# A routed two-layer block on one core: the router reads raw sums, token remainders move to TensorE and ScalarE

## The reference

```
x = layernorm(ALPHA * x + attention(x), ln_g[layer, 0], ln_b[layer, 0])
f = grouped_moe(x, router_w, router_b, w_gate, w_up, w_down)
x = layernorm(ALPHA * x + f, ln_g[layer, 1], ln_b[layer, 1])

def grouped_moe(x, ...):
    scores = sigmoid(x @ router_w)                 # 256 x 32
    sel = scores + router_b                        # choose by these
    # the group of 4 experts whose two best sum highest, then its two best experts
    gate = scores of the two, divided by their sum
    y += gate_e * ((silu(x @ w_gate[e]) * (x @ w_up[e])) @ w_down[e])   # e chosen for the token
```

## Time and profile before

| | us |
|---|---|
| three runs | 733.11, 728.86, 729.58 |
| median | 729.58 |
| the profiled execution | 729.95 |
| its span, first to last instruction | 728.1 |
| mean granted clock of TensorE | 0.984 |
| busy in the span: TensorE, VectorE, ScalarE, GpSimd | 686.7, 335.1, 211.2, 129.5 |

### The profile page before, as it was taken

The page is one execution under the profiler, slowest core; times in us unless marked ns, Lnnn a source line. Parts: engine busy times, 40 slices in busy tenths (PEclk is TensorE's granted clock), DMA queues, the critical chain, the costliest instruction groups (busy, mean ns, idle before and its releaser), DMA issues. The chain is left out here.

```text
span 728.1 us, 10053 instructions
## 1 busy us (share of the span) xinstructions
PE 686.7 (94%) x3657; PEld 382.6 (53%) x3657; DVE 335.1 (46%) x672; ACT 211.2 (29%) x416; POOL 129.5 (18%) x141
## 2 busy tenths in 40 slices
PE   7999999879999999999989898988999999999993
PEld 5979778453334343345546776845433434334551
DVE  4758654753433324233264755585343432323226
ACT  4568661312111111111155135341211111111111
POOL 4004010140201010010019560015120101001000
PEclk9999999999999999999999999999999999999998
DMA  8980058929999999999995019393999999999991
GB/s 310 385 338 2 1 216 368 406 85 361 420 421 422 421 421 421 421 424 420 423 417 232 1 33 421 131 387 111 367 421 421 420 422 421 423 420 423 420 413 66
DMA packets 40360, 237.65 MB, mean 326 GB/s; under 512 B 3825, under 2 KB 4257, under 8 KB 15233
## 3 DMA queue, kind: packets, MB, share of 16 engines
q1 hardware_dynamic: 39408, 235.64, 79.5%
q10 hardware_dynamic: 576, 1.05, 0.5%
q0 software_dynamic: 336, 0.44, 0.2%
HBM read 236.06 MB, written 1.05 MB: 326 GB/s over the span
## 5 line engine op out<-in xcount | busy, mean ns | idle before, releaser
L572 PE MATMUL psum<-ring,work 128*64 128x512 f32 (+2 forms) x1296 | 234.0, 512 | 7.2 <-DVE work L1981 7.2
L572 PEld LDWEIGHTS psum<-ring,work 128*64 128x64 f32 (+1 forms) x1296 | 95.5, 140 | 143.0 <-issue 119.7
L572 PE MATMUL psum<-ring,scratch 128*64 128x512 f32 x512 | 116.9, 598 | 3.7 <-ACT scratch L1440 3.7
L2023 DVE TENSOR_TENSOR scratch<-psum,scratch 128x256 f32<-128x256 f32 x32 | 13.6, 425 | 183.2 <-ACT scratch L1436 183.2
L2099 POOL COPY work<-work 128x512 f32 x60 | 39.0, 651 | 316.5 <-PE psum L572 307.6
L1429 ACT ACTIVATE x_T_rounded<-psum,small 128x512 fp32r<-128x512 f32 x64 | 43.8, 687 | 110.2 <-DVE scratch_rounded L2004 75.8
L572 PEld LDWEIGHTS psum<-ring,scratch 128*64 128x64 f32 x512 | 33.9, 136 | 68.8 <-issue 63.6
L1436 ACT ACTIVATE scratch<-psum 128x256 f32<-128x256 f32 x32 | 12.3, 384 | 195.1 <-PE psum L572 195.1
L572 PE MATMUL psum<-ring_rounded 128*128 128x256 f32 (+1 forms) x214 | 66.5, 311 | 0.0
L572 PE MATMUL psum<-ring_rounded,x_T_rounded 128*128 128x512 f32 x192 | 60.6, 396 | 0.0
L572 PE MATMUL psum<-x_T_rounded,scratch_rounded 128*128 128x512 f32 x128 | 56.7, 443 | 0.9 <-issue 0.7
(11 more groups left out here) (247 smaller groups left out, 845.9 us busy)
## 6 DMA issues: line engine op xcount, KB each, us to landing
ring<-in_moe_w_gate SPq DMA_DIRECT2D x64, 1024.0 KB, 15.4
ring<-in_moe_w_up SPq DMA_DIRECT2D x64, 1024.0 KB, 19.6
ring<-in_moe_w_down SPq DMA_DIRECT2D x64, 1024.0 KB, 20.2
ring<-in_diff_w_qkv SPq DMA_DIRECT2D x5, 2048.0 KB, 19.9
ring<-in_diff_w_o SPq DMA_DIRECT2D x1, 4096.0 KB, 14.5
ring<-in_mla_w_o SPq DMA_DIRECT2D x1, 4096.0 KB, 35.9
ring<-in_mla_w_q_b SPq DMA_DIRECT2D x1, 2304.0 KB, 29.5
ring<-in_mla_w_kv_b SPq DMA_DIRECT2D x1, 2048.0 KB, 28.0
```

Source lines behind the costliest of these rows:

```text
L572: return pe.matmul(dst, lhsT, rhs, start=start, stop=stop, skip_group_check=True)
L2023: dve.tensor_tensor(h_sb, psum[:, 6, FF:2 * FF], act_s, ALU.mult).then_inc(m["h_ready"], 1)
```

## The change

- **Raw sums to the router.** TensorE transposes `xs` before it is normalised, as soon as the addition of a tile is done (`z_ready`), each tile into two banks of its own. ScalarE and VectorE copy one bank each of a tile (`raw_copy`) without scale and shift. No zero matmuls stand ahead of the transposes.
- **The norm on the logits.** The router's weights are multiplied by the norm's scale (`rw_scaled`) and by its shift, and both are summed by column (`router_rows`); a product with ones spreads the sums to all tokens. A logit becomes `rstd` times the raw one, plus the shift's sum, minus mean times `rstd` times the scale's sum: two VectorE instructions a tile, the second ahead of the sigmoid.
- **Normalisation later.** ScalarE normalises tile 0 after the logit copy and tile 1 after the sigmoid, each whole; VectorE's half is gone.
- **Remainders.** `tok_hi` and `tok_lo` keep the tokens' own order of columns; the casts read without a step, and the sort takes every eighth column as its stationary operand. TensorE forms `xs` times the identity (fp32) plus `hi` times the negative identity in two banks, and ScalarE copies that to `tok_lo`. VectorE's three subtractions are gone. `TOP_WAIT` is 6 instead of 28.
- **Diagonals.** `tok_lo[1]` lies where `diag` lies, so GpSimd now waits for the whole sort (`sort_ps`) before it writes `diag`.
- **Queues.** The router's weights are issued by GpSimd behind the squares (layer 0) and behind the split weights (layer 1). SyncE reads the overflow count of layer 0 into a register ahead of the attention's loads instead of behind them.

```diff
-START_WAIT, FIRST_WAIT, TOP_WAIT, SORT_WAIT = 14, 8, 28, 8
-NORM_WAIT = {1: (8, 4), 2: (11, 0), 3: (8, 4)}
+RAW_BANKS = ((4, 5, 2, 3), (4, 5, 6, 7))
+ROW_BANK = (6, 3)
+REST_BANK = (4, 6)
+START_WAIT, FIRST_WAIT, NORM_WAIT, TOP_WAIT, SORT_WAIT = 14, 8, (11, 0), 6, 8
...
-            load_router(0)
+            sp.wait_ge(*at[0]("o_ps", HEADS))
             load_down(0, 0, 0)
...
+            more = overflows(sp, 0)
             sp.wait_ge(*mo[0]("gu_ps", 14))
...
# TensorE, moe(l)
-                transpose_x(2 * l + 1)
-                pe.wait_ge(ld_rw, 16 * (l + 1))
+                for t in range(TT):
+                    pe.wait_ge(z_ready, TT * l + t + 1)
+                    for half in range(2):
+                        for k in range(4):
+                            last = pe.transpose(psum[:, RAW_BANKS[l][2 * t + half], k * P:(k + 1) * P],
+                                                xs[:, t, 4 * half + k::KD], ident)
+                        last.then_inc(xt[2 * l + 1]["ps"], 1)
+                mm(psum[:, ROW_BANK[l], 0:2 * EXPERTS], ones, routing()["rows"], True, True).then_inc(m["lg_ps"], 1)
+                pe.wait_ge(*x_copied(2 * l + 1))
...
-                    last = mm(psum[rows, 0, 0:SEQ], rw[:, k, :], xT[:, k, :], k < 4, k >= 4)
+                    last = mm(psum[rows, 0, 0:SEQ], rw_scaled[:, k, :], xT[:, k, :], k < 4, k >= 4)
...
-                keep_clock(TOP_WAIT)
+                for t in range(TT):
+                    banks = [psum[:, REST_BANK[t] + c, :] for c in range(2)]
+                    cols = [slice(c * 512, (c + 1) * 512) for c in range(2)]
+                    pe.wait_ge(*ln[2 * l]("norm", (1, 3)[t]))
+                    for c in range(2):
+                        mm(banks[c], ident, xs[:, t, cols[c]], True, False)
+                    pe.wait_ge(*m("hi_ready", t + 1))
+                    for c in range(2):
+                        last = mm(banks[c], minus_ident[:, :], tok_hi[t][:, cols[c]], False, True)
+                    last.then_inc(m["lo_ps"], 1)
+                keep_clock(TOP_WAIT, 0)
...
-                    for half, part in enumerate(xs_parts(t, k)):
-                        last = mm(psum[:, SORT_BANKS[k], :], part, onehot_r[:, t, :],
+                    for half, part in enumerate((tok_hi[t], tok_lo[t])):
+                        last = mm(psum[:, SORT_BANKS[k], :], part[:, k::KD], onehot_r[:, t, :],
...
+                pe.wait_ge(*m("lo_ready", TT))
                 for t in range(TT):
-                    pe.wait_ge(*m("hi_ready", t + 1))
                     pe.wait_ge(*m("hot_ready", t + 1))
-                    pe.wait_ge(*m("lo_ready", t + 1))
...
# ScalarE, moe(l)
-                act_xt(2 * l + 1)
+                root(n, 0)
+                raw_copy(0)
+                root(n, 1)
+                raw_copy(1)
                 act.activation(small[:, 60:61], eps[:, :], ACT.Sigmoid)
-                act.wait_ge(*m("lgt_ps", 1))
-                act.copy(logit_T, psum[:, 0, 0:SEQ]).then_inc(m["lgt_sb"], 1)
-                act.wait_ge(*m("lg_ps", 1))
-                act.activation(routing()["score"], psum[:, 1, 0:64], ACT.Sigmoid).then_inc(m["score"], 1)
-                act.wait_ge(*ln[2 * l]("norm", 3))
+                act.wait_ge(*m("lg_ps", 2))
+                act.copy(logit_T, psum[:, 0, 0:SEQ]).then_inc(m["router_act"], 1)
+                normalise(0)
+                act.wait_ge(*m("logit", TT))
+                act.activation(routing()["score"], routing()["sel"], ACT.Sigmoid).then_inc(m["router_act"], 1)
+                normalise(1)
+                act.wait_ge(*ln[n]("norm", 3))
                 act.wait_ge(*m("hi_ready", 1))
-                act.copy(hi_1, xs_tiles(1, 0, KD)).then_inc(m["hi_ready"], 1)
+                act.copy(tok_hi[1], xs[:, 1, :]).then_inc(m["hi_ready"], 1)
+                for t in range(TT):
+                    act.wait_ge(*m("lo_ps", t + 1))
+                    act.copy(tok_lo[t], psum[:, REST_BANK[t]:REST_BANK[t] + 2, :].rearrange("p c n -> p (c n)"))\
+                       .then_inc(m["lo_ready"], 1)
...
# VectorE, raw_layer_norm (new; router_rows(l) is called just before it)
+                statistics(n, 1)
+                raw_copy(0)
+                raw_copy(1)
+                scales(n, 1)
+                dve.wait_ge(*ln[n]("rstd", TT))
+                dve.wait_ge(*m("lg_ps", 1))
+                row = c["rows"]
+                chain(dve.tensor_copy(row, psum[:, ROW_BANK[l], 0:2 * EXPERTS]))
+                for t in range(TT):
+                    part = slice(t * EXPERTS, (t + 1) * EXPERTS)
+                    last = dve.scalar_tensor_tensor(out=c["masked"][:, part], in0=row[:, 0:EXPERTS],
+                                                    scalar=ln_nb[:, t:t + 1], in1=row[:, EXPERTS:2 * EXPERTS],
+                                                    op0=ALU.mult, op1=ALU.add)
+                chain(last)
+                dve.wait_ge(*m("lg_ps", 3))
+                for t in range(TT):
+                    part = slice(t * EXPERTS, (t + 1) * EXPERTS)
+                    dve.scalar_tensor_tensor(out=c["sel"][:, part], in0=psum[:, 1, part], scalar=ln_rstd[:, t:t + 1],
+                                             in1=c["masked"][:, part], op0=ALU.mult, op1=ALU.add)\
+                       .then_inc(m["logit"], 1)
...
# VectorE, moe(l)
-                dve_xt(2 * l + 1)
-                dve.wait_ge(*m("hi_ready", 1))
-                dve.tensor_tensor(lo_0, xs_tiles(0, 0, KD), hi_0, ALU.subtract).then_inc(m["lo_ready"], 1)
...
-                chain(dve.tensor_tensor(lo_1[0], xs_tiles(1, 0, 4), hi_1[:, 0:4, :], ALU.subtract))
-                dve.tensor_tensor(lo_1[1], xs_tiles(1, 4, KD), hi_1[:, 4:KD, :], ALU.subtract)\
-                   .then_inc(m["lo_ready"], 1)
...
# GpSimd
-                pool.tensor_copy(hi_0, xs_tiles(0, 0, KD)).then_inc(m["hi_ready"], 1)
+                pool.tensor_copy(tok_hi[0], xs[:, 0, :]).then_inc(m["hi_ready"], 1)
...
                 pool.wait_ge(*m("key_ready", 1))
+                pool.wait_ge(*m("sort_ps", KD))
...
+            load_router(0)
             moe(0)
```

136 lines of the change are left out of this document (79 added, 57 removed).

## The result

| | us |
|---|---|
| five runs | 722.91, 724.67, 722.67, 725.16, 723.02 |
| median (forecast 721.5, range 716 to 728) | 723.02 |
| ratio to the kernel before | 0.992, 95% interval 0.9897 to 0.9944 |
| the profiled execution, its span | 722.91, 721.1 |
| busy in the span: TensorE, VectorE, ScalarE, GpSimd | 679.4, 331.2, 212.4, 129.6 |

A forecast was written before the change was run, and what follows sets the result against it. TensorE and the DMA engines bound the expert loops; VectorE is the path from projection to gate. Gains of 12.5 less costs of 4.4 net 8.1 us: 721.85, or 721.5 against the median; own range 717.5 to 725.5, wider range 716 to 728.

The forecast's parts named there:

- From the projection to the selection: Output projection's end to selection start: transposing raw sums starts the selection earlier, gaining 2.6 us in layer 0, 2.4 in layer 1.
- TensorE late in layer 0: Selection's end in layer 0: TensorE's 28 zero matmuls outlast the selection; being on time gains 1.3 us.
- The clock on the remainder piece: TensorE's remainder products and zero matmuls ahead of the counts: low clock expected in both layers, costing 1.6 us each, 3.2 total.
- Remainders: Both remainder subtractions leave VectorE ahead of keys, offsets and copies: 2.24 us a layer gained one to one, 4.5 in all.
- VectorE stays last, by a microsecond: From sort start S to gate: VectorE needs S + 9.5; last sorted bank ready S + 7.4, copied by S + 8.2.
- Diagonals: GpSimd's diagonals, now waiting for the sort, run beside VectorE's window copies: cost 0.6 us a layer, 1.2 in all.
- Gate's own clock: Gate 0 takes 5.36 us against 3.67 at low clock after a pause; slowdown taken as gone in one layer, gaining 1.7.
- Router load: Router's weights on GpSimd's queue: issued at 105, landed at 113, row sums done before 118.4, at no cost.
- rival C: Late router weights: landing 18.3 us after issue delays VectorE's first addition, last statistics 3.4 late; 724.9 us, chance 0.08.
- Nothing elsewhere: Expert loops: nothing there can be shortened by changing the routing; what lies ahead shifts each loop as a whole.

The follow-up runs named there:

- cast_act: Changed kernel with tile 0's rounding cast on ScalarE, between the sigmoid and tile 1's normalisation, instead of on GpSimd: median 721.43 us, ratio 0.9913 to the kernel before.
- norm_first: Changed kernel with the old front back (both tiles normalised ahead of the transposes), remainders still on TensorE and ScalarE: median 725.85 us, ratio 0.9949 to the kernel before.
- before_again: The kernel before the change, unedited, run again for a second profile: median 729.14 us, ratio 0.9997.
- packed_sort: Changed kernel with the sort's stationary tiles as 128 adjacent columns instead of every eighth (sorted features wrong): median 719.76 us, ratio 0.9879 to the kernel before.
- free_diag: Changed kernel with GpSimd's diagonals in free memory, so they start with the keys, not the sort's end: median 722.04 us, ratio 0.9904 to the kernel before.
- load_sync: Changed kernel with the router's weights loaded through SyncE's queue again, ahead of pair 0's down weights: median 729.21 us, ratio 0.9984 to the kernel before.
- rest_vector: Changed kernel with tile 1's remainder formed by VectorE again, as one contiguous subtraction behind the one-hots: median 727.01 us, ratio 0.9971 to the kernel before.
- lo_packed: Changed kernel with diagonals in free memory, tile 0's cast on ScalarE, two pre-count zero matmuls, and only the sort's remainder tile packed: 721.29 us, ratio 0.989.

## Why the prediction was right, and where by luck

The time was forecast at 721.5 and is 723.0; the sum of 8.1 stands against 7.0 in the profiled span, and 6.6 and 5.4 by the two medians. Its terms fit less well than the sum.

- **From the projection to the selection, 2.6 and 2.4.** Start right: counted from the end of the projection's last row, as the prediction counts, 5.94 and 5.95 (6.2 forecast), so 2.9 and 2.6 gained; router products 2.91 (3.2 forecast). But the selection did not keep its length: 0.57 went to the port that VectorE shares with GpSimd, whose cast I had not followed when its norm moved beside the selection (cast_act). With that, the raw front is worth 2.1 a layer (norm_first).
- **TensorE late in layer 0, 1.3.** This was a spell of the one execution that I read, and no part of the kernel (before_again). The profile before already had layer 1 as the counterexample, 6.21.
- **The clock on the remainder piece, 3.2.** Place and size of the slow piece right (1.48 more in tile 0's two identity products), its price too high: VectorE was itself 0.57 late, so a spell costs 0.7 ahead of the counts, and it came in at most one of the two layers in each profile but one.
- **Remainders, 4.5.** 1.9 too much. VectorE's 2.24 went from its order one to one, but from the sort's start to the gate only 1.3 a layer was gained (10.14 and 10.13 against 11.54 and 11.31). The step that failed is "VectorE stays last, by a microsecond": the sort ended at S + 8.2, not S + 7.4, and its end became what the last copy waits for. Of that, 0.64 is the strided loads (packed_sort ends at S + 7.55). packed_sort has the gate at S + 9.50, the lower end of the forecast; but with its last copy waiting 0.29 in layer 1 and not at all in layer 0 it has no microsecond of margin either.
- **Diagonals, 1.2.** Sum right by luck (0.6 a layer, free_diag), place wrong: 0.1 on VectorE's copies, far under the 0.6 that they were given, and 0.44 in a wait of the row products, which I had covered with 1 us. That microsecond was counted with a start at S + 7.4 and a length of 4.67; they started at S + 8.4 and took 5.82.
- **Gate's own clock, 1.7 in one layer.** Gone in both in the first profile, in neither in the second, so the one that was forecast is a mean and no reading; 1.17 each where it goes, as the wait for the diagonals comes back.
- **Router load, no cost.** Right, and what carries it is the queue: rival C was worked out at 3.4 and the delay and the spell behind it took 4.9 (load_sync). Forecast landing 113, row sums at 111.93.
- **Nothing elsewhere.** The expert loops shift as a whole: from layer 0's up product to the last product of its pairs 201.40 to 201.43 in all profiles. The 2.2 outside of them were not foreseen: 0.75 behind the last pair, cause open, the rest a second spell in the latent attention.

So gains of 9.7 in the two fronts, more than forecast since the profile before had two gates and a run of zero matmuls at low clock and the one after only one spell; and 2.7 given back where nothing was changed. Part of the fit is cancellation: too much for the remainders and for a spell that was no property of the kernel, against too high a price for the clock.

## What to carry to other kernels

Where work is taken from the engine that is last, cost the one behind it with its new operands and not its old period: here the change that freed VectorE also put a step of 32 bytes on the sort's weights, and 0.64 us a layer went there. Before a slow stretch of the profile is counted as a gain, look for the same stretch in the other layer or in a second profile; most spells of low clock moved between two profiles of one kernel, and one in the latent attention hardly did. That a longer pause calls one up is a guess that no run here tested. A transfer that must land before a fixed time belongs on a queue without bulk loads ahead of it, and an instruction moved in time should be checked against the neighbour whose port it shares.

## What the runs showed of the hardware

- A step of eight fp32 elements cost TensorE on both operands, by different amounts: a 128x128 load of the sort 0.33 instead of 0.19 us, of which the sort's period shows 0.018 (0.245 against 0.227); fp32 products of 512 moving columns about twice (3.85 against 1.88 for two). The Trainium skill (SBUF — State Buffer, section "Door 1: The DMA port swizzle") says that each access that crosses to a new line of 16 bytes pays a penalty; the trace agrees in both places and disagrees in a third: the transposes load fp32 columns with the same step in 0.19.
- The same step costs ScalarE's cast 2.03 instead of 1.03 when it reads SBUF, and nothing when it reads PSUM and writes packed (1.01).
- VectorE's subtraction of 1024 columns: 1.22 contiguous, 2.28 with the step.
- The granted clock fell in different stretches in the two profiles of each kernel (remainder products, gate, latent attention), and in the kernel before four times of four in a gate behind a pause of 3.4 to 3.7 us. No length of pause decides it: the zero matmuls ahead of the sort were slow in both layers of rest_vector (3.34 and 3.36 instead of 1.89), with a pause of 3.06 ahead of the counts, and in both of lo_packed (2.78), with one of 0.97. Tile 0's two identity products took 3.43 to 3.75 where such a spell fell on them and 1.95 at the upper level.
